# A transformer-like diffusion block in exact-split fp32r: the moving operands and the weight rings begin at other places in SBUF

## What is computed

```python
def swiglu(h, w_in, w_out):
    gu = h @ w_in                                  # 1024 -> 2 * 2816
    g, u = jnp.split(gu, 2, axis=-1)
    return (jax.nn.silu(g) * u) @ w_out            # 2816 -> 1024
...
def trunk_layer(x, xc, mod, mod_c, p, ctx_out):
    x = ffn_sublayer(x, mx[0:3], p["norm_ffn1"], p["w_ffn1_in"], p["w_ffn1_out"])
    xc = ffn_sublayer(xc, mc[0:3], p["norm_ffn1"], p["w_ffn1_in"], p["w_ffn1_out"])
    x, xc = mixer_sublayer(x, xc, mx[3:6], mc[3:6], p, ctx_out)
    x = ffn_sublayer(x, mx[6:9], p["norm_ffn2"], p["w_ffn2_in"], p["w_ffn2_out"])
    if ctx_out:
        xc = ffn_sublayer(xc, mc[6:9], p["norm_ffn2"], p["w_ffn2_in"], p["w_ffn2_out"])
```

## The kernel before

| tensor | before | past a multiple of 2048 | after the change | past a multiple of 2048 |
|---|---|---|---|---|
| x | 16512 | 128 | 18432 | 0 |
| h_hi | 32896 | 128 | 34816 | 0 |
| h_lo | 49280 | 128 | 51200 | 0 |
| raw, w_lo | 65664 | 128 | 67648 | 64 |
| w_hi | 82048 | 128 | 84032 | 64 |
| ada | 98432 | 128 | 102400 | 0 |
| buf_a | 106624 | 128 | 110592 | 0 |
| buf_b | 110720 | 128 | 114688 | 0 |
| masks | 120448 | 1664 | 124416 | 1536 |
| a_hi | 133088 | 2016 | 135168 | 0 |
| a_lo | 178144 | 2016 | 180224 | 0 |
| ba_hi | 198624 | 2016 | 200704 | 0 |
| ba_lo | 202720 | 2016 | 204800 | 0 |

## Time and profile before

### The profile page before, as it was taken

The page is one execution under the profiler, slowest core; times in us unless marked ns, Lnnn a source line. Parts: engine busy times, 40 slices in busy tenths (PEclk is TensorE's granted clock), DMA queues, the critical chain, the costliest instruction groups (busy, mean ns, idle before and its releaser), DMA issues.

```text
span 2314.8 us, 33776 instructions
## 1 busy us (share of the span) xinstructions
PE 2216.4 (96%) x12654; PEld 1859.2 (80%) x12654; DVE 1371.3 (59%) x2301; ACT 885.8 (38%) x1375; POOL 218.8 (9%) x287
## 2 busy tenths in 40 slices
PE   6999999999999999999999999999999998898998
PEld 3888878987558777888887888888889777788998
DVE  4778876533456457478875256655256555665554
ACT  3433312533444325342322253332244552355553
POOL 0001112000001200301101100000110001101001
PEclk8999999999999999999999999999999999899999
DMA  6455554422112205345554344444333311144555
GB/s 260 154 190 197 189 180 128 134 82 83 41 41 69 69 28 202 117 164 197 189 189 124 96 127 148 145 140 141 94 127 119 107 51 54 58 162 146 181 174 153
DMA packets 96912, 303.86 MB, mean 131 GB/s; under 512 B 10672, under 2 KB 17328, under 8 KB 95920
## 3 DMA queue, kind: packets, MB, share of 16 engines
q1 hardware_dynamic: 77520, 232.96, 30.9%
q0 software_dynamic: 18720, 69.21, 8.8%
q10 hardware_dynamic: 576, 0.34, 0.0%
HBM read 291.99 MB, written 10.49 MB: 131 GB/s over the span
## 4 chain that ended last, share of the span: by engine, by line
PE 56%; DVE 4%; ACT 2%; DMA 1%; issue 1%; DVEq 0%; ACTq 0%; SPq 0%
PE ps L2034 16%; PE ps L2036 16%; PE ps L2035 16%; DVE w_lo L1448 1%; PE ps L2285 1%; PE ps L2306 1%; PE ps L2400 1%; PE ps L2403 1%; PE ps L2411 1%; PE ps L2470 0%; PE ps L2472 0%; PE ps L2222 0%; PE ps L2294 0%; DMA raw<-in_w_down 0%; ACT w_hi L824 0%
## 5 line engine op out<-in xcount | busy, mean ns | idle before, releaser
L2034 PE MATMUL ps<-h_hi,w_hi 128*128 128x512 f32 (+1 forms) x2176 | 777.4, 357 | 30.5 <-DVE w_lo L1448 13.4
L2036 PE MATMUL ps<-h_hi,w_lo 128*128 128x512 f32 (+1 forms) x2176 | 760.2, 349 | 0.0
L2035 PE MATMUL ps<-h_lo,w_hi 128*128 128x512 f32 (+1 forms) x2176 | 760.1, 349 | 0.0
L1448 DVE TENSOR_TENSOR w_lo<-raw,w_hi 128x1024 fp32r<-128x1024 f32 (+2 forms) x416 | 476.1, 1148 | 468.8 <-ACT w_hi L824 463.4
L824 ACT ACTIVATE w_hi<-raw 128x1024 fp32r<-128x1024 f32 (+2 forms) x416 | 404.7, 975 | 624.1 <-DMA raw<-in_w_down 317.2
L2034 PEld LDWEIGHTS ps<-h_hi,w_hi 128*128 128x128 f32 x2176 | 417.7, 192 | 120.6 <-issue 42.5
L2036 PEld LDWEIGHTS ps<-h_hi,w_lo 128*128 128x128 f32 x2176 | 417.9, 192 | 51.9
L2035 PEld LDWEIGHTS ps<-h_lo,w_hi 128*128 128x128 f32 x2176 | 418.4, 192 | 48.4
L2034 PE MATMUL ps<-a_hi,w_hi 128*128 128x512 f32 (+1 forms) x1050 | 362.1, 345 | 10.6 <-DVE buf_b L1911 4.4
L2036 PE MATMUL ps<-a_hi,w_lo 128*128 128x512 f32 (+1 forms) x1050 | 360.9, 344 | 0.0
L2035 PE MATMUL ps<-a_lo,w_hi 128*128 128x512 f32 (+1 forms) x1050 | 359.3, 342 | 0.0
(11 more groups left out here) (259 smaller groups left out, 1822.8 us busy)
## 6 DMA issues: line engine op xcount, KB each, us to landing
raw<-in_w_up SPq DMA_DIRECT2D x176, 512.0 KB, 3.8
ada<-in_w_ada_t POOLq DMA_DIRECT2D x128, 512.0 KB, 3.9
raw<-in_w_down SPq DMA_DIRECT2D x64, 384.0 KB, 3.2
raw<-in_w_gate SPq DMA_DIRECT2D x48, 512.0 KB, 3.5
raw<-in_w_down SPq DMA_DIRECT2D x64, 320.0 KB, 2.9
raw<-in_w_proj SPq DMA_DIRECT2D x32, 512.0 KB, 3.3
raw<-in_w_merge SPq DMA_DIRECT2D x16, 512.0 KB, 3.7
raw<-in_w_out SPq DMA_DIRECT2D x16, 512.0 KB, 3.3
```

What stands on the lines that cost most here:

```text
L1448: vec.tensor_tensor(w_lo[:, j % RING, 0:cols], raw[:, j, 0:cols], w_hi[:, j % RING, 0:cols].bitcast(F32), ALU.subtract).then_inc(s_lo, 1)
L2034: pe.matmul(out, wh, rows_hi[:, i, c], start=first, stop=False)
L2035: pe.matmul(out, wh, rows_lo[:, i, c], start=False, stop=False)
L2036: return pe.matmul(out, wl, rows_hi[:, i, c], start=False, stop=last)
```

## The change

The small tensors that stood behind `masks` are asked for first, with eight floats of padding (`pad_rows`), so that x and both halves of h begin at a multiple of 2048 bytes. `pad_weights` puts 64 bytes ahead of the weight rings, and `pad_rest` the missing 1984 bytes behind them, so that all that follows up to `masks` and, with the rest of the small tensors, both halves of a begin at a multiple of 2048 again. The instructions of every engine, their order, their waits and all transfers stay as they are; only addresses differ.

```diff
+        ones = sb("ones", [P, P])
+        eps_col = sb("eps_col", [P, 1])
+        one_col = sb("one_col", [P, 1])
+        vecs = sb("vecs", [P, DEPTH, N_VEC])
+        nfin = sb("nfin", [P, KD])
+        c_in = sb("c_in", [P, KD, 2])
+        c_act = sb("c_act", [P, KD, 2])
+        ada_sum = sb("ada_sum", [P, 4])
+        scale_first = sb("scale_first", [P, KD, 2])
+        sb("pad_rows", [P, 8])
         x = sb("x", [P, KD, TOK])
         with ExitStack() as s:
             gate_in = sb("gate_in", [P, 4, 3, TOK], at=s)
         h_hi = sb("h_hi", [P, KD, TOK], F32R)
         h_lo = sb("h_lo", [P, KD, TOK], F32R)
+        sb("pad_weights", [P, 16])
         with ExitStack() as s:
             raw = sb("raw", [P, RING, KD * P], at=s)
         w_lo = sb("w_lo", [P, RING, KD * P], F32R)
         w_hi = sb("w_hi", [P, RING, KD * P], F32R)
+        sb("pad_rest", [P, 496])
         ada = sb("ada", [P, 2, KD * P])
...
         gate_sums = nc.dram_tensor("gate_sums", (DEPTH, N_GATE, P, TOK), F32, kind="Internal")
-        ones = sb("ones", [P, P])
-        eps_col = sb("eps_col", [P, 1])
-        one_col = sb("one_col", [P, 1])
-        vecs = sb("vecs", [P, DEPTH, N_VEC])
-        nfin = sb("nfin", [P, KD])
-        c_in = sb("c_in", [P, KD, 2])
-        c_act = sb("c_act", [P, KD, 2])
-        ada_sum = sb("ada_sum", [P, 4])
-        scale_first = sb("scale_first", [P, KD, 2])
         mod_rest = sb("mod_rest", [P, ADA_REST // 2, 4])
```

## The result

The changed kernel takes 2324.81 us (median of 12 runs) where the kernel before takes 2314.31 us (12 runs beside them): ratio 1.0044, 95% interval 1.0031 to 1.0057. Its profiled execution spans 2322.6 us, 7.8 more than before.

A forecast was written before the change was run, and what follows sets the result against it. PE's product pace was taken to set 1769 of 2314.8 us. Gains of 90.6 us, less 4.5 (mixers), 3 (waits) and 2 (low clock), left 81: 2313.5 - 81 = 2232.5, say 2233; range 2205 to 2325.

The forecast's parts named there:

- What bounds the kernel: PE, busy 96% of the span; its own pace in the products sets 1769 us of 2314.8.
- rival D: All h products: 0 apart is best, 64 as bad as 32; 233.2 ns, +25 us, 2338; chance 0.18.
- the new relation of 64 apart: h and a against the weight rings: one common pace, 217 ns for 512 columns and 114 for 256.
- (1): h and rings moved to 64 apart; 512-column h products: 3888 x (226.8 - 217) = 38.1 us gained.
- (2): a moved to 64 apart from the rings; 512-column a products: 1698 x (233.2 - 217) = 27.5 us gained.
- (3): As used here, the 256-column products: 4092 x (120 - 114) = 24.6 us; the prediction's own part of this number was ba.
- ba: Products with h moving, weights now 0 apart from h: 226.8 in place of 234.5 ns for 48 matmuls, 0.4 us.
- A: The forecast itself, all products: standing 64 apart takes the two reads mostly off each other; 2206 to 2273 us; chance 0.43.
- B: Only a split over a 64-byte boundary costs: h stays, a falls to 226.8 ns; 11.3 us, 2302; chance 0.21.
- C: The change does nothing to the products' pace, the extra being the array's own at the high clock; 2313; chance 0.14.
- The other engines' 1%: Shifted places on DVE and ACT cost nothing; at most 1% of DVE's 1371 us, 14 us.
- the growth of waits: PE's waits for w_lo (17.0 us) and h_lo (15.0) rise as PE arrives earlier; 3 us taken off for h_lo.

The follow-up runs named there:

- 77 pairs: Bare three-matmul products without the rest of the kernel, at 77 different pairs of starts of moving rows and weights; none under 226.7 ns (512 columns) or 113.3 (256).
- rings_only: The kernel before with both weight rings 64 bytes further and x, h and a unmoved: 2323.15 us, ratio 1.0057 (1.0032 to 1.0082).
- M=32 W=32: Bare products, moving rows (M) and weights (W) both beginning 32 bytes past a multiple of 2048: 226.7 ns at 512 columns, 120.0 at 256.
- M=16 W=32: Bare products, moving rows 16 and weights 32 bytes past a multiple of 2048: 236.7 / 233.3 ns at 512 columns in two orders, 117.3 / 116.9 at 256.
- M=0 W=48: Bare products, moving rows at a multiple of 2048 and weights 48 bytes past one: 123.3 ns, given as the dearest at 256 columns.

## Why the prediction was wrong

**What bounds the kernel** was read rightly: the paces of PE carry it, and the span of every kernel above follows from the table of mean steps within 5 us. Right too was that a and h would get one common pace at 512 columns: it came, at the wrong end (233.3). The count of h products fell to 858, next to the 860 that the prediction had named as the sign of rival D.

**The step that failed** is the price of the new relation of 64 apart, "I take 217 ns for 512 columns and 114 for 256". At 512 columns it measured 233.3 ns, the upper of the two ends taken from the trace, not near the lower. The reason given for the lower half (one-column matmuls whose loads go at 112 ns) was a row of another kind: it has no long stream beside the load, and so says nothing of the two together. The 13 ns that h showed were not what a bad relation costs but what the best one costs: 226.7 was the lowest 512-column pace in 77 pairs. At 256 columns the 114 agrees with the measured 114.7 and 115.7, but in part by luck: it came from the same reasoning that failed at 512, and the mean depends on which of two paces, 113.3 or 117.8, the long stretches fall into (116.6 and 117.1 in rings_only). The picture behind it, that 64 apart takes two colliding reads off each other, is not borne out: at 512 columns the new place added 6.5 ns, and narrower loads did not remove the extra.

With 233.3 in the sum, (1) is 3888 x (226.8 - 233.3) = -25 us in place of +38.1, (2) is 0 in place of +27.5, (3) 24.6 becomes 19.3, and ba gives its 0.4 or less (its pace came to 227.8 in place of 234.1): that is 6 us slower, against 10.5 measured between the medians. Pauses and the clock add 2.7 us in the profiled executions; the rest is not assigned. That the time still lies just within the stated 2205 to 2325 is luck: that range was drawn without the mechanism that came, and 19.3 us at 256 columns brought it back inside.

**The rivals.** D named the mechanism and its price at 512 columns to 0.1 ns (0 apart is the best relation for h, a stays where it was), and its point of decision, 228.7 ns, was passed. Its time of 2338 was 13 us too high; it held 256 columns at 120 ns, which is 19 us too much by the paces. Two halves of different rivals were true at once: A's at 256 columns and D's at 512. I had given one relation one quality for both widths; nothing in the rows said that. B's ground (a split 64-byte line) is refuted by M=32 W=32, though its sum for a, 11.3 us, is what comes where all are 0 apart (11.1). C is out: the places do change the pace.

**The page's rules.** TensorE: Matmul & The Clock Gate in the Trainium skill says in step 1 of Part 2 that loading the next weights does not steal read bandwidth from the running matmul. If that is taken to mean that the load leaves the matmul's pace alone, it does not hold here for fp32r: bare products change from 226.7 to 233.3 ns by the load's address alone. Whether read bandwidth is what is lost, no run here shows. The same page's N/2.4 + 2.5 ns (Back-to-back issue gap) agrees to 0.1 ns with the bf16 groups, 215.8 and 109.2, and falls short of every fp32r group with 128-column loads, by 10.9 ns or more at 512 columns and by 4.1 or more at 256.

**The other terms.** The other engines' 1% and the growth of waits were nothing (17.1 and 14.9 us against 17.0 and 15.0), as PE did not become faster over the whole.

## What to carry to other kernels

An extra of some ns in a pace is not evidence that it can be removed: before pricing a new relation of addresses from the ones in a trace, sweep it in a bare program, which costs one run and here repeated the kernel's paces within 0.4 ns. Give each width of moving operand its own line in such a sweep, since the best place at 512 columns (0 apart, 226.7) is among the slow ones at 256 (120 where 113.3 is to be had). When a change moves several tensors, undo them one by one: here a's move was worth 11 us with the rings where h needs them, and nothing with the rings 64 bytes on.

## What the runs showed of the hardware

An fp32r product with a weight load of its own costs, at the high clock, 13.3 ns over its stream at best for 512 columns (226.7 against 213.3) and 6.7 at best for 256 (113.3 against 106.7). By the place of its operands it costs up to 23 and 17 (236.7 at M=16 W=32, 123.3 at M=0 W=48). With M at a multiple of 32, the relation W - M counts modulo 256, within some 1 ns at 512 columns and 1.6 ns at 256 (apart from the two paces of 64 apart); where M is 8, 16 or 24 past such a multiple, its own place counts as well. In bf16, at the two relations tried, none of it shows.

One relation can have two steady paces (113.3 and 117.8 at 64 apart). The same pair took one pace in one order and the other in the other, and in the kernels a stretch keeps its pace until the next pause, so what ran just before seems to decide. That it is the phase of the two reads after a pause is my reading, which was not tried alone. What collides is still open: loads of a quarter of the columns do not make the extra smaller at 512 columns and 0 apart (231.7 against 226.7), though they do at 256 (113.3 or 117.8 against 120).
